# Five feed-forward blocks: a distance of the high plane and an order of the couples for each

## What is computed

```python
def swiglu(h, w_gate, w_up, w_down):
    return (jax.nn.silu(h @ w_gate) * (h @ w_up)) @ w_down

# first network, layer 0 (width D_FF_DENSE = 2816)
h = h + swiglu(rms_norm(h, ln_ffn[layer]), e_ffn_w_gate[j], e_ffn_w_up[j], e_ffn_w_down[j])

# second network, each of two layers (width D_FF = 2816)
h = rms_norm_2(x, ffn1_norm[l])
x = x + 0.5 * swiglu_ffn(h, ffn1_w_gate[l], ffn1_w_up[l], ffn1_w_down[l])
...
h = rms_norm_2(x, ffn2_norm[l])
x = x + 0.5 * swiglu_ffn(h, ffn2_w_gate[l], ffn2_w_up[l], ffn2_w_down[l])
```

## Time and profile before

| | us |
|---|---|
| median of 3 runs | 2395.82 |
| lowest, highest | 2395.14, 2395.85 |
| the profiled execution's own time | 2395.84 |
| its span, first to last instruction | 2393.7 |
| PE busy | 2371.1 (99%) |
| VectorE busy | 1877.3 (78%) |
| ScalarE busy | 1439.7 (60%) |

### The profile page before, as it was taken

How to read it: one execution, slowest core, us unless ns; L and a number is a source line. 1 busy time by engine, 2 the same in 40 slices (tenths; PEclk the granted TensorE clock), 3 DMA queues, 4 the chain that set the end, 5 groups by cost and what they waited for, 6 DMA issues and landing times.

```text
span 2393.7 us, 34175 instructions
## 1 busy us (share of the span) xinstructions
PE 2371.1 (99%) x12542; PEld 2012.4 (84%) x12542; DVE 1877.3 (78%) x1961; ACT 1439.7 (60%) x1474; POOL 14.3 (1%) x34
## 2 busy tenths in 40 slices
PE   8999999999999999999999999999999999999998
PEld 7788899888888888888888888888888888897887
DVE  7767786678888888888889898677966677788766
ACT  6645455467777777777777776555254454544444
POOL 1000000000000000000000010000000000000000
PEclk9999999999999999999999999999999999999999
DMA  8375233459999999999999996853455666533663
GB/s 302 111 258 177 70 131 141 152 202 376 382 379 348 381 379 378 348 381 377 380 348 378 381 395 249 281 180 124 132 188 181 194 229 230 177 128 123 199 192 126
DMA packets 315953, 603.73 MB, mean 252 GB/s; under 512 B 9121, under 2 KB 135201, under 8 KB 315553
## 3 DMA queue, kind: packets, MB, share of 16 engines
q1 hardware_dynamic: 314160, 592.70, 69.9%
q10 hardware_dynamic: 1136, 7.87, 0.8%
q0 software_dynamic: 576, 2.10, 0.2%
HBM read 597.91 MB, written 8.91 MB: 254 GB/s over the span
## 4 chain that ended last, share of the span: by engine, by line
PE 94%; DVE 3%; ACT 1%; DMA 1%; DVEq 1%; issue 0%; SPq 0%; ACTq 0%
PE bank L217 20%; PE bank L219 19%; PE bank L218 19%; PE bank L1229 17%; PE bank L1234 8%; PE bank L3526 1%; PE bank L2968 1%; PE bank L3453 1%; PE bank L2243 1%; PE bank L2253 1%; DMA mslot<-in_e_w_in 1%; PE bank L2943 1%; PE bank L1727 1%; PE bank L1070 0%; PE bank L2162 0%
## 5 line engine op out<-in xcount | busy, mean ns | idle before, releaser
L3218 DVE TENSOR_TENSOR weights_lo<-mslot,weights_hi 128x2048 fp32r<-128x2048 f32 x336 | 767.5, 2291 | 112.8 <-ACT weights_hi L3111 112.1
L3111 ACT ACTIVATE weights_hi<-mslot 128x2048 fp32r<-128x2048 f32 x336 | 644.1, 1920 | 212.9 <-PE bank L219 212.8
L1229 PE MATMUL bank<-x_parts,weights_hi 128*128 128x512 f32 x1760 | 510.3, 393 | 1.9 <-DVE x_parts L933 1.9
L1383 DVE TENSOR_TENSOR weights_lo<-scratch,weights_hi 128x2048 fp32r<-128x2048 f32 x165 | 377.2, 2289 | 164.4 <-ACT weights_hi L1376 164.4
L1229 PEld LDWEIGHTS bank<-x_parts,weights_hi 128*128 128x128 f32 x1760 | 325.2, 188 | 71.3 <-DVE x_parts L933 2.4
L217 PE MATMUL bank<-weights_hi,x_parts 128*128 128x512 f32 x920 | 359.7, 391 | 1.0 <-DVE weights_lo L3218 0.7
L217 PE MATMUL bank<-weights_hi,x_pair 128*128 128x512 f32 x896 | 354.8, 396 | 0.2 <-issue 0.2
L219 PE MATMUL bank<-weights_hi,x_pair 128*128 128x512 f32 x896 | 349.8, 390 | 0.0
L218 PE MATMUL bank<-weights_lo,x_pair 128*128 128x512 f32 x896 | 349.3, 390 | 0.0
L218 PE MATMUL bank<-weights_lo,x_parts 128*128 128x512 f32 x888 | 346.1, 390 | 0.0
L1234 PE MATMUL bank<-x_parts,weights_lo 128*128 128x256 f32 x1760 | 343.3, 280 | 0.0
(11 more groups left out here) (551 smaller groups left out, 2625.2 us busy)
## 6 DMA issues: line engine op xcount, KB each, us to landing
mslot<-in_o_moe_w_gate SPq DMA_DIRECT2D x112, 1024.0 KB, 6.4
mslot<-in_o_moe_w_up SPq DMA_DIRECT2D x112, 1024.0 KB, 6.3
mslot<-in_o_moe_w_down SPq DMA_DIRECT2D x112, 1024.0 KB, 6.6
scratch<-in_ffn_w_gate SPq DMA_DIRECT2D x44, 1024.0 KB, 5.4
scratch<-in_ffn_w_up SPq DMA_DIRECT2D x44, 1024.0 KB, 5.4
scratch<-in_ffn_w_down SPq DMA_DIRECT2D x44, 1024.0 KB, 5.2
mslot<-in_o_w_in SPq DMA_DIRECT2D x7, 2048.0 KB, 10.6
scratch<-in_e_ffn_w_gate SPq DMA_DIRECT2D x11, 1024.0 KB, 5.4
```

The lines of the kernel that those rows point to most:

```text
L1229: pe.matmul(m.ps[bank + j][:, :].rearrange("p (i t) -> p i t", i=2), hi[:, k, cols(j)], m.x_wide[k], start=(k == 0), stop=False)
L1383: dve.tensor_tensor(m.wlo[to][:, :], m.fslot[i], m.whi[to][:, :], ALU.subtract).then_inc(m.sig["f_lo"], 1)
L3111: act.activation(m.whi[(place + half) % PLACES][:, :], r.slot[slot + half], ACT.Copy).then_inc(s["r_hi"], 1)
L3218: dve.tensor_tensor(m.wlo[i][:, :], r.slot[slot + half], m.whi[i][:, :], ALU.subtract).then_inc(s["r_lo"], 1)
```

## The change

Each of the five blocks gets its own distance of the high plane, in XH_AT: 0, 112, 0, 48 and 16 columns, or 0, 448, 0, 192 and 64 bytes, for blocks 0 to 4. Block 3 keeps what it had. m.x_wide and m.f_xh become lists with an entry for each block, and every user picks its block's.

Each block also gets its own order, in IN_TURNS. Blocks 0, 1 and 4 keep theirs (couples while the second column block's wides are made). Blocks 2 and 3 get couples in both column blocks: wide(0, k), narrow(0, k) for the eight k, and then the same for tile 1. In these the wait for the low weights stands ahead of the first wide.

m.x2 now spans exactly two planes, and r.yh and r.yl begin at column 2048, 48 columns (192 bytes) earlier. The number of instructions of each kind stays the same.

```diff
-XH_AT = PIECE + 48
+XH_AT = [PIECE + at for at in (0, 112, 0, 48, 16)]
+IN_TURNS = (1, 1, 2, 2, 1)
...
-    m.x2 = x_all[:, 0:XH_AT + PIECE]
-    planes = x_all[:, 0:2 * XH_AT].rearrange("p (i t) -> p i t", i=2)
-    m.x_wide = [planes[:, :, k * SEQ:(k + 1) * SEQ] for k in range(KT)]
-    m.f_xl, m.f_xh = cut(x_all, 0, KT, SEQ), cut(x_all, XH_AT, KT, SEQ)
+    m.x2 = x_all[:, 0:2 * PIECE]
+    planes = [x_all[:, 0:2 * at].rearrange("p (i t) -> p i t", i=2) for at in XH_AT]
+    m.x_wide = [[t[:, :, k * SEQ:(k + 1) * SEQ] for k in range(KT)] for t in planes]
+    m.f_xl, m.f_xh = cut(x_all, 0, KT, SEQ), [cut(x_all, at, KT, SEQ) for at in XH_AT]
...
-            pe.matmul(m.ps[bank + j][:, :].rearrange("p (i t) -> p i t", i=2), hi[:, k, cols(j)], m.x_wide[k],
+            pe.matmul(m.ps[bank + j][:, :].rearrange("p (i t) -> p i t", i=2), hi[:, k, cols(j)], m.x_wide[v][k],
...
-                last = pe.matmul(m.ps[bank + j][:, 0:SEQ], lo[:, k, cols(j)], m.f_xh[:, k, :],
+                last = pe.matmul(m.ps[bank + j][:, 0:SEQ], lo[:, k, cols(j)], m.f_xh[v][:, k, :],
...
+            return
+        if IN_TURNS[v] == 2:
+            split_in(kind, u)
+            if row_scale:
+                rows_spread()
+            for j in tiles:
+                for k in range(KT):
+                    wide(j, k)
+                    last = narrow(j, (k,))
+                last.then_inc(s[done], 1)
             return
         for k in range(KT):
             wide(0, k)
...
-    r.yh, r.yl = (x2[:, XH_AT + i * KT * P:XH_AT + (1 + i) * KT * P] for i in range(2))
+    r.yh, r.yl = (x2[:, (2 + i) * KT * P:(3 + i) * KT * P] for i in range(2))
```

More of the change, by code:

```diff
@@ L933, in ffn_entry_low @@
         dve.scalar_tensor_tensor(m.f_xl[:, k, :], turned(m, u, k),
-                                 gain[:, k:k + 1], m.f_xh[:, k, :], ALU.mult, ALU.subtract).then_inc(s["n_xl"], 1)
+                                 gain[:, k:k + 1], m.f_xh[m.splits[u]][:, k, :], ALU.mult, ALU.subtract).then_inc(s["n_xl"], 1)
 def ffn_entry_dve(dve, m, u, gain, v, scale):
@@ L1027, in tokens @@
             act.wait_ge(s["n_tr"], rows_turned(m, u) + k // 2 + 1)
-            last = act.activation(m.f_xh[:, k, :], turned(m, u, k), ACT.Copy, scale=gain[:, k:k + 1])
+            last = act.activation(m.f_xh[m.splits[u]][:, k, :], turned(m, u, k), ACT.Copy, scale=gain[:, k:k + 1])
             if k % 2 == 1:
@@ L1285, in down_part @@
         hi, lo = parts(ffn_place(v, "down", NU - 1 if final else None), D)
-        hh, hl = ffn_hidden(m, last=final)
+        hh, hl = ffn_hidden(m, v, last=final)
         cols, tok = slice(half * HALF, (half + 1) * HALF), slice(t * P, (t + 1) * P)
@@ L1335, in ffn_pe, with ffn_hidden @@
         norm_pe(pe, m, u_out, 0)
-def ffn_hidden(m, last):
+def ffn_hidden(m, v, last):
     if last:
-        pair = [t[:, KT - 2:KT, :].rearrange("p k t -> p (k t)") for t in (m.f_xh, m.f_xl)]
+        pair = [t[:, KT - 2:KT, :].rearrange("p k t -> p (k t)") for t in (m.f_xh[v], m.f_xl)]
     else:
@@ L1468, in hidden @@
     def hidden(u, last=False):
-        hh, hl = (flat(t) for t in ffn_hidden(m, last))
+        hh, hl = (flat(t) for t in ffn_hidden(m, v, last))
         for j, cols in enumerate(halves):
```

## The result

The changed kernel takes 2404.39 us (median of 5 runs, 2403.81 to 2405.54), against 2395.85 us for the kernel before (2395.14 to 2396.39): ratio 1.0036, 95% interval 1.0021 to 1.0051, or 8.5 us slower. My forecast was 2394.9 us, with a range up to 2400.5. The profiled run took 2403.92 us, with a span of 2401.9.

What follows compares the result with a forecast made beforehand. The prediction took TensorE's back-to-back matmuls as the bound; +1.1 (order) + 1.75 (wait) + 0.2 (late couples) - 4.0 (distance) = -0.95 us against 2395.82 us gave 2394.9 us, range 2390.5 to 2400.5 us.

Steps and rivals of the forecast that it cites:

- What bounds the kernel: Whole kernel: TensorE's matmuls one after another; floor 227 and 113 ns, 340 ns a couple; margin 9.4 us, 0.4%.
- Part 1, the order: Blocks 2 and 3: all 16 couples alternate at 347 ns, 0.05 us more an up piece, +1.1 us.
- Part 2, the wait: Block 3's first up piece: TensorE waits for the low parts, no longer covered by 8 wides; +1.75 us.
- The +0.2 us for couples at 360 ns behind a late wait: Final up piece of blocks 2 and 3: couples may run at 360 ns; bounds 0 and 0.4, +0.2 us taken.
- Part 3, the distance: High plane's new distance in blocks 0, 1, 2 and 4: part of the margin comes back, -4.0 us.
- half of the best case: Blocks 0, 1, 4 and 2 all going to the floor would give 8.0 us; half taken, -4.0 us.
- the nearest row for a distance of 0 is the down product: Ground for part 3: down product reads from the same 512-byte boundaries without a gap and is at the floor.
- today's price: For 448 and 64 bytes, blocks 1 and 4: the nearest price is the present one, no gain at all.
- the sign of a wrong forecast: Any block: a piece moving by more than 0.11 us, or TensorE waiting at more places than the one named.
- Rival 1: The distance does nothing, couples keep 347 ns, only parts 1 and 2 count: 2398.9 us; chance 0.28.
- Rival 2: Everything reaches the floor, block 3's couples as well: -7.4 us, 2388.4 us; chance 0.12.
- Rival 3: Blocks 2 and 3: couples stay at 360 ns behind the wait, 8.7 us on top, 2407.6 us; chance 0.12.

Runs made afterwards that it cites:

- the wait covered: Against the changed kernel: all distances 192 bytes, each block's first up piece in the old order; 2396.97 us, ratio 1.0006.
- The shifted run: Against the changed kernel: old order, distances 192, 0, 64, 128, 192 bytes, weight parts and planes all 192 bytes further on; 2412.53 us, single execution.
- the best version found: 192 bytes everywhere; against the version with 2 couples in up and 3 in gate pieces, 5 in gate and last up pieces; 2391.86 us, ratio 0.9986.

## Why the prediction was wrong

**What bounds the kernel** was right: PE alone, and a margin of a few nanoseconds a matmul over a floor of 227 and 113 ns. No trace went under the floor.

**Part 1, the order: right.** Forecast +1.1 us for the two blocks. From gate(1) to the last up matmul a block took 160.00 us in the new order at 192 bytes (block 2 with the wait covered, block 3 in the changed kernel), against 159.43 and 159.49 in the kernel before: +1.1 us.

**Part 2, the wait: right.** Forecast +1.75 us at block 3's first up piece. In the changed kernel the way from block 3's first matmul to its second gate piece grew from 12.97 to 14.76 us, by 1.79 us. The place, the covering wides and the fact that no other place of these blocks waits for its low parts were all read correctly. The +0.2 us for couples at 360 ns behind a late wait was not spent in the changed kernel (its last up piece in block 2 took 5.661 us, 0.02 over the others), but was in block 2 of the run with the order alone. What I missed here is the clock: in one trace 1.9 us of an idle TensorE were followed by 3.4 us at half of it, another 1.7 us.

**Part 3, the distance: wrong in sign, and this is the step that failed.** I took half of the best case, -4.0 us. Measured: +1.77 in block 0, +0.03 in block 1, +1.65 in block 4, and in block 2 162.31 - 160.00 = +2.31 us from gate(1) on in the new order (+1.82 for the block in the old one, in the run with the distances alone), +5.8 us together. The term is 9.8 us off, which is the whole miss (9.5). The reasoning failed at "the nearest row for a distance of 0 is the down product". All of the -4.0 hung on it, as blocks 0 and 2 at the floor are 4.2 us. In that product the roles are the other way round: the weights are the moving operand and the hidden values the stationary one, and the low ones lie in another buffer. The shifted run showed that it is at the floor only by such a place itself. Couples at a distance of 0 cost 353 ns, not 340. What I called today's price was right for 448 bytes, and for the wrong reason: it is the place modulo 256 bytes that repeats, not a neighbourhood. For 64 bytes it was wrong by 1.65 us. Block 2's up piece moved by 0.15 us, over the 0.11 that I had named as the sign of a wrong forecast. And I had a bound of +11.3 us for this term and let the range end 4.7 us above the kernel before. With an effect of unknown sign, of which the trace of before holds a single sample, taking half of the gain as the middle and cutting the loss short had no ground in a row.

**The rivals.** Rival 1 (the distance does nothing) is refuted by blocks 0 and 4. Rival 2 (all to the floor) never came near; even the best version found keeps 0.08 us over the floor in a pair of pieces. Rival 3 had the sign but another mechanism: the couples of blocks 2 and 3 did not stay at 360 ns, and cost 353 where the distance was 0 and 347 where it was 192. By the rule that PE's two read ports are independent and PE never waits on anyone (the Trainium skill, SBUF — State Buffer, "Who interferes with whom") an address can't matter. These traces do not agree: the same matmuls on the same data went from 347 to 353 ns a couple when only an address changed by 192 bytes, and what counts is the place of the moving operand against the stationary one. Whether it is the two reads that meet is not shown.

**What stays open.** Which rhythm of the memory or of the array makes the pace and hands it on from one run of matmuls to the next, and whether the weight load behind a matmul or its own stationary operand is the partner. All runs say how the pace moves; none isolates the two reads.

## What to carry to other kernels

Where TensorE is busy without a gap, read the distance between starts, not the duration, and look for runs of the same matmul at two paces: that is a margin, here about 9 us of 2396, and in this kernel it went by the place of the moving operand against the stationary one and by what ran before. No row of the kernel before told which place is cheap, so measure it: give one kernel as many settings as it has equal stages and read them all from one trace; five blocks gave five distances a run. Before a wait is moved ahead of independent matmuls, look for the one place where they covered it; it cost 1.8 us here for a gap of 1.9, and an idle TensorE may cost clock as well.

## What I had not expected of the hardware

- The price of the same piece depends on addresses, and repeats modulo 256 bytes to the nanosecond; gate and up took 5.607/5.588 us at 0, 256 and 512 bytes, 5.577/5.594 at 64 and 320, 5.640/5.586 at 128 and 384, 5.555/5.492 at 192 and 448.
- The pace is carried. At 192 bytes wides run at 227 or 230 ns and narrows at 113 or 118, for the whole run, by how it was entered; in couples the wide goes 234, 231, 228 in turn, and only behind a 234 do narrows run at 113. Choosing the number of couples by that made the loop pieces 10.96 us a pair instead of 11.05. At other distances the sequence is another (233, 241, 236 in the couples at 0 bytes).
- An idle gap of 1.91 us on TensorE was followed by 3.4 us at half the clock in one trace, and one of 1.93 us by none in the trace of the changed kernel.
